# Modulation rows for GpSimd: four buffers in place of two, other places in the load order, and the gates' logarithm behind the first key chunk

## What is computed

```python
mod = silu(c) @ mod_w[l] + mod_b[l]              # 1024 x 6144, one row vector
sh1, sc1, g1, sh2, sc2, g2 = split(mod, 6)
h = rmsnorm(x, norm_g) * (1 + sc1) + sh1
proj = h @ w_in                                   # q, k: 512; v, og: 1024; gl: 16
log_a = log_sigmoid(gl @ w_g2 + b_g2) / 16        # the gates' logarithm
b = cumsum(log_a)                                 # inside chunks of 64 tokens
q_t, k_t, k_dec = q * exp(b), k * exp(-b), k * exp(b_last - b)
y = (chunked attention, normed, * silu(og)) @ w_out
x = x + g1 * y
h = rmsnorm(x, norm_g) * (1 + sc2) + sh2          # and so on
```

## Time and profile before

| | |
|---|---|
| median of 3 runs | 3109.04 us (3103.89 to 3110.97) |
| profiled execution | 3110.73 us, span 3108.9 us |
| PE busy | 2952.2 us, 95% |
| DVE busy | 2079.2 us, 67% |
| ACT busy | 1598.0 us, 51% |
| POOL busy | 1342.1 us, 43% |
| granted PE clock, mean | 0.974 |

### The profile page before, as it was taken

How to read it: one execution, slowest core, us unless ns; L and a number is a source line. 1 busy time by engine, 2 the same in 40 slices (tenths; PEclk the granted TensorE clock), 3 DMA queues, 4 the chain that set the end, 5 groups by cost and what they waited for, 6 DMA issues and landing times.

```text
span 3108.9 us, 59282 instructions
## 1 busy us (share of the span) xinstructions
PE 2952.2 (95%) x19024; PEld 2681.0 (86%) x19024; DVE 2079.2 (67%) x3812; ACT 1598.0 (51%) x3132; POOL 1342.1 (43%) x1069
## 2 busy tenths in 40 slices
PE   7999999988999998999999899999899999999998
PEld 6679999986787877899999777887799889999997
DVE  7646963358888877589203888888655447777776
ACT  1225554478555555555555865554564335455554
POOL 5823988886544410069888855444000010000100
PEclk8999999999999998999999999999999999999998
DMA  6534556731666632445567046665454345555553
GB/s 243 213 101 152 182 196 245 275 122 54 250 233 229 232 123 72 131 156 183 181 207 257 24 150 254 238 232 193 135 181 133 120 131 192 194 190 201 189 195 122
DMA packets 153464, 552.60 MB, mean 178 GB/s; under 512 B 16896, under 2 KB 19712, under 8 KB 153232
## 3 DMA queue, kind: packets, MB, share of 16 engines
q1 hardware_dynamic: 151136, 547.42, 51.5%
q10 hardware_dynamic: 2224, 3.87, 0.4%
HBM read 550.17 MB, written 1.05 MB: 177 GB/s over the span
## 4 chain that ended last, share of the span: by engine, by line
PE 60%; issue 20%; POOL 9%; ACT 7%; DVE 3%; DMA 1%; POOLq 0%; ACTq 0%; SPq 0%; DVEq 0%
PE bank L1002 20%; PE bank L1282 12%; PE bank L1032 10%; PE bank L1303 6%; PE bank L743 5%; ACT hT L1514 3%; PE bank L795 3%; POOL w_parts L2642 1%; POOL mean L2690 1%; POOL hT L2690 1%; ACT hT L1510 1%; POOL mean L2692 1%; POOL hT L2692 1%; ACT h_parts L1522 1%; PE bank L767 1%
## 5 line engine op out<-in xcount | busy, mean ns | idle before, releaser
L2642 POOL TENSOR_TENSOR w_parts<-ring,w_parts 128x512 fp32r<-128x512 f32 x512 | 660.9, 1308 | 419.3 <-ACT w_parts L1474 392.0
L1002 PE MATMUL bank<-h_parts,w_parts 128*128 128x256 f32 x6144 | 750.1, 284 | 7.0 <-POOL w_parts L2642 7.0
L1002 PEld LDWEIGHTS bank<-h_parts,w_parts 128*128 128x128 f32 x6144 | 741.7, 192 | 8.0 <-POOL w_parts L2642 5.5
L1474 ACT ACTIVATE w_parts<-ring 128x512 fp32r<-128x512 f32 x512 | 320.0, 631 | 343.3 <-PE bank L1002 238.1
L1695 ACT ACTIVATE w_parts<-ring 128x512 fp32r<-128x512 f32 x384 | 242.3, 632 | 266.0 <-PE bank L1282 171.2
L1282 PEld LDWEIGHTS bank<-h_parts,w_parts 128*128 128x128 f32 x3072 | 374.5, 193 | 3.9 <-DVE arena L2504 1.5
L1282 PE MATMUL bank<-h_parts,w_parts 128*128 128x256 f32 x3072 | 375.4, 284 | 1.4 <-DVE arena L2504 1.4
L1032 PE MATMUL bank<-w_parts,a_parts 128*128 128x512 f32 x1536 | 372.2, 398 | 2.4 <-DVE a_parts L2278 2.3
L2573 DVE TENSOR_TENSOR w_parts<-ring,w_parts 128x512 fp32r<-128x512 f32 x376 | 272.5, 736 | 147.5 <-ACT w_parts L1695 144.1
L1032 PE MATMUL bank<-h_parts,a_parts 128*128 128x512 f32 x1536 | 364.1, 392 | 6.6 <-DVE a_parts L2278 6.6
L1032 PEld LDWEIGHTS bank<-h_parts,a_parts 128*128 128x128 f32 x1536 | 285.2, 188 | 78.8 <-DVE a_parts L2278 20.6
(11 more groups left out here) (348 smaller groups left out, 4302.6 us busy)
## 6 DMA issues: line engine op xcount, KB each, us to landing
ring<-stream SPq DMA_DIRECT2D x786, 512.0 KB, 3.4
arena<-stream SPq DMA_DIRECT2D x144, 512.0 KB, 4.4
hT<-stream SPq DMA_DIRECT2D x80, 512.0 KB, 4.5
mean<-stream SPq DMA_DIRECT2D x32, 512.0 KB, 4.5
arena<-consts ACTq DMA_DIRECT2D x1, 1536.0 KB, 6.4
xT<-xin ACTq DMA_DIRECT2D x1, 1024.0 KB, 10.8
out<-hT SPq DMA_DIRECT2D x4, 256.0 KB, 2.2
arena<-subk ACTq DMA_DIRECT2D x2, 128.0 KB, 2.2
```

Of the source, the lines that this page charges most:

```text
L1002: mm = pe.matmul(bank[k][:, 0:T], w[:, wp, ws], h_parts[:, hp, 4 * j + q, :], start=(j == 0 and q == 0 and i == 0), stop=(j == 1 and q == ...
L1474: act.activation(w_parts[half % HALVES][:, 0, :], ring[slot_][:, j * 512:(j + 1) * 512], ACT.Copy).then_inc(sem(f"{n}_high"), 1)
L2642: pool.tensor_tensor(w[:, 1, :], ring[(base + k) % RING][:, j * 512:(j + 1) * 512], w[:, 0, :].bitcast(F32), ALU.subtract).then_inc(sem(f" ...
```

## The change

The 24 rows of POOL get four buffers (at 0, 1, 5 and 6 x 1024 of the arena), each with its own semaphore. The later groups of rows keep two. The two new buffers are those of DVE's first products, so from the third row on the load waits until DVE has made all nine of its rows (`first_made`), and from the fifth on it waits until the row four before it is made. In the list `at` the rows stand behind slots 17, 18, 19, 21, 22, 23, 25, ... (three rows for four slots) up to 42 for the twentieth, and the last four behind slot 43; before, they stood behind slots 8, 10, 14, 17, then two for three slots from 18 to 37, and six behind 43. In ACT's order the gates' sigmoid and logarithm come behind the eviction of the first key tile, not behind that of the fourth.

```diff
-        mod_landed = [sem("mod_landed0"), sem("mod_landed1")]
+        mod_landed = [sem(f"mod_landed{i}") for i in range(4)]
+        N_GLA = MODS_GLA[1] - MODS_GLA[0]
+
+        def mod_lane(j):
+
+            return j % 4 if j < N_GLA else j % 2
+
+        def mod_arrival(j):
+
+            return 16 * (j // 4 + 1) if j < N_GLA else 16 * ((j - N_GLA) // 2 + N_GLA // 4 + 1)
...
-                return arena[:, 0:CH], arena[:, CH:2 * CH]
+                return tuple(arena[:, i * CH:(i + 1) * CH] for i in (0, 1, 5, 6))
...
                 j = mod_number(m)
-                if m >= seg[0] + 2:
-                    sp.wait_ge(sem("mod_made"), j - 1)
-                sp.dma_start(mod_buffers(seg)[j % 2], stream[mod_row(m)]).then_inc(mod_landed[j % 2], 16)
+                lanes = len(mod_buffers(seg))
+                if m >= seg[0] + lanes:
+                    sp.wait_ge(sem("mod_made"), j - lanes + 1)
+                elif m >= seg[0] + 2:
+                    sp.wait_ge(sem("first_made"), len(SUMMED_MODS))
+                sp.dma_start(mod_buffers(seg)[mod_lane(j)], stream[mod_row(m)]).then_inc(mod_landed[mod_lane(j)], 16)
...
-            at = [8, 10, 14, gla + 1] + [gla + 2 + 3 * i // 2 for i in range(14)] + [gla + 27] * 6
+            at = [gla + 1 + 4 * i // 3 for i in range(20)] + [gla + 27] * 4
...
-            for h in range(GH):
-                copy_act(act, G.k[:, h, :], f"g_k{h}")
-
+            copy_act(act, G.k[:, 0, :], "g_k0")
             act.wait_ge(sem("g_abs"), 1)
             act.activation(G.e, G.e, ACT.Sigmoid, scale=-1.0).then_inc(signal("g_act"), 1)
             act.wait_ge(sem("g_act"), signalled("g_act"))
             act.activation(G.e, G.e, ACT.Ln).then_inc(signal("g_ln"), 1)
             act.wait_ge(sem("g_ln"), signalled("g_ln"))
+            for h in range(1, GH):
+                copy_act(act, G.k[:, h, :], f"g_k{h}")
...
-            pool.wait_ge(mod_landed[j % 2], 16 * (j // 2 + 1) if it is None else it * 32 + 16 * (j // 2 + 1))
+            pool.wait_ge(mod_landed[mod_lane(j)], mod_arrival(j) if it is None else it * 32 + mod_arrival(j))
```

More of the change, by code:

```diff
@@ L2684, in mod_pool @@
         def mod_pool(pool, seg, i, j, c_b, it=None):
-            buf, part = mod_buffers(seg)[j % 2], mod_parts(seg)[i % len(mod_parts(seg))]
+            buf, part = mod_buffers(seg)[mod_lane(j)], mod_parts(seg)[i % len(mod_parts(seg))]
             b3 = buf.rearrange("p (k n) -> p k n", k=DC)
             step = lambda k: 3 * j + k if it is None else it * 12 + (3 * j + k)
-            pool.wait_ge(mod_landed[j % 2], 16 * (j // 2 + 1) if it is None else it * 32 + 16 * (j // 2 + 1))
+            pool.wait_ge(mod_landed[mod_lane(j)], mod_arrival(j) if it is None else it * 32 + mod_arrival(j))
             pool.tensor_tensor(b3, b3, c_b, ALU.mult).then_inc(sem("mod_step"), 1)
```

## The result

| | before | changed |
|---|---|---|
| median | 3108.35 us (20 runs, 3102.19 to 3114.98) | 3117.73 us (20 runs, 3109.22 to 3123.31) |
| ratio | | 1.0028, 95% interval 1.0020 to 1.0035 |
| span of the profiled execution | 3108.9 us | 3117.2 us |
| granted PE clock, mean | 0.974 | 0.971 |

The forecast was 3104.8, between 3098 and 3111, with 6% for slower. The time lies outside the range and on the other side.

What follows compares the result with a forecast made beforehand. POOL's last row was taken to bound the output projection's start, at 178.9 instead of 183.10. The 4.2 us gained gave 3106.5 for the profiled execution and 3104.8 for the median, range 3098 to 3111.

Steps and rivals of the forecast that it cites:

- (a): Head, without POOL rows or loads: VectorE's first rows done 8.9 us earlier, first projection at 43.1 instead of 53.19.
- (b): Rope arguments after the norm: VectorE queues behind POOL, TensorE waits 3.5 us at the fourth query tile, plus 1.7 clock.
- (c): Four buffers for POOL's rows: its seventh row starts at 78.3, and from there POOL has no gap.
- (d): Gates' logarithm moved earlier: price and gain 0; without it VectorE's chain would end at 138, still ahead of TensorE.
- (e): POOL's last 18 rows: 81.7 us alone, 15.7 more beside VectorE's chain, 0.8 for later operations; last row at 176.5.
- (f): Gate projection: slot 40 lands at 135.1, TensorE wants it at 135.6, so the stall at 133.7 is gone.
- The sum: Output projection: TensorE could start at 173.3, POOL allows 178.9; the later counts, gaining 4.2 us on 183.10.
- my rivals: Four alternatives: no rope wait (0.27), POOL no bound (0.06), first projection unmoved (0.10), POOL ending at 178 to 180.
- Rival 3: First projection does not move, so POOL's late start is pure loss: 5.9 us later, 3114.9; chance 0.10.
- the heart of the case: Before the output projection: TensorE finishes POOL's last columns, then waits 1.77 us for VectorE, a margin of 1.8 us.

Runs made afterwards that it cites:

- e1: Changed kernel with VectorE's two scalings of the output gates moved behind its first four state copies; ratio to the kernel before 1.0012.
- e7: Kernel before with only the gates' logarithm moved behind the first key eviction; ratio to the kernel before 0.9999.
- e4: Changed kernel with the gates' logarithm put back behind the fourth key eviction; ratio to the kernel before 1.0012.
- e2: Changed kernel with seven useless 256-column matmuls on TensorE ahead of the state loop's second chunk, where it waits; ratio to the kernel before 1.0003.
- e6: Changed kernel with ScalarE's rope sines behind its first five evictions and VectorE's output-gate scalings behind the first state copies; ratio to the kernel before 0.9983.
- e10: Kernel before with only VectorE's output-gate scalings moved behind the first state copies; ratio to the kernel before 1.0002.
- e3: Kernel before with two extra maxima on VectorE between the output-gate scalings and the first state copies, to make TensorE wait; ratio to the kernel before 1.0050.
- e5: Changed kernel with ScalarE's two rope sines put behind its first five evictions; ratio to the kernel before 1.0008.

## Why the prediction was wrong, step by step

*(a) The head* was right: 8.9 us forecast, 10.1 with the gain operation, 9.2 to 11.4 measured (the upper bound was 11).

*(b) The rope collision* was right in its mechanism, and mis-sized. Of the 19 operations 14 met POOL, one for one; the first ran just ahead, and four in POOL's gap. This is VectorE in the changed kernel:

```profile
47.30 2.90 DVE L1954 SCALAR_TENSOR_TENSOR arena<-arena 128x256 f32<-128x256 f32 x3
50.23 1.87 DVE L1896 TENSOR_SCALAR arena<-arena 128x256 f32<-128x256 f32 x1
...
55.00 0.29 DVE L1900 TENSOR_SCALAR arena<-arena 128x256 f32<-128x256 f32 x1
...
56.31 2.00 DVE L1898 TENSOR_TENSOR rope_c<-rope_c,arena 128x256 f32<-128x256 f32 x1
```

An operation that takes 0.29 us in POOL's gap takes 1.87 behind POOL's longest one. The wait was forecast at 3.5 us and was 4.7 to 7.9. It has these two sizes because POOL's fourth row lands in the middle of the last operations: in e1 it lands after a gap of 0.67 us and catches six, in the changed kernel after 1.33 and catches four. I had three. With four caught the arguments were ready 19.2 us behind the start of the first projection, forecast 18.9; most of the 1.2 us over the forecast is that TensorE asked for the bank after 16.0 us and not after 16.9. With six caught, the wait is 7.8 to 7.9, beyond my bound (five caught, 2 us more).

*(c), (d)* were right in their own terms: POOL waited for no load behind the start of its seventh row (78.6, forecast 78.3), and the logarithm alone is worth nothing in the kernel before (e7). Without this edit the chain would have ended at 144.2 and not at my 138 (e4), 1 us before TensorE asked for it. But I looked at the end of VectorE's chain only, and its place decides also which of POOL's operations stands where the scalings begin (e4).

*(e) POOL's total.* The last 18 rows take 98.3 to 98.5 us in all six profiles with this load order and the sines in their old place; 98.2 was forecast. The last row came at 176.9 in the profiled execution of the changed kernel (forecast 176.5) and at 179.3 to 182.4 in the other five, since the seventh row started anywhere from 78.6 to 84.1, by the wait of (b) and by the start of the first projection. The profiled one had the earliest start of the six, 41.75 where 43.1 was forecast, so that its last row fits so well is in part luck. Behind it the last columns take 3.9 us and not 2.4, since a TensorE that waits for POOL does them at 1.2 GHz. POOL's bound is then at 180.8 to 186.3 and not at 178.9; e1, e2 and e4 show 183.2 and 186.3, which is no gain over 183.10.

*(f)* was right: no stall, or 1 us at most, at the gate projection.

*The sum* is where it failed: "could start the output projection 34.3 later". I took TensorE's path behind the gate projection over from the kernel before, at full clock, and it took 51.1 us (138.93 to 190.02). In (e) I had put 0.8 us of contention on POOL for VectorE's later operations, these scalings among them, and had not asked what the meeting costs VectorE, nor who waits for VectorE there. The price in the profiled execution was copies 2.1 us late, 1.5 us of wait, and 13.5 us in the state loop through the clock (0.9 and some 11 in its two other profiles); the 8 us or so that TensorE had to spare ahead of POOL's last row (8.06 of wait in e1) hid a part of it. Even without this loss nothing of the forecast gain of 4.2 us is left (e1, e2 and e4: 1.0003 to 1.0012), through the wait of (b) and the last columns of (e). Of the changed kernel's 8.7 us (0.28%), e1 gives back 5.0 and e6 another 9, more than all of it.

None of my rivals was this one. Rival 3, the only one on the slower side, has the first projection unmoved, and it moved about as forecast. What I called the heart of the case, POOL's margin of 1.8 us, was real but second.

The Trainium skill (SBUF — State Buffer, Who interferes with whom) has the rule that issue order decides who blocks; the trace agrees both times (1.87 us behind POOL, and POOL's 512-element halving at 1.59 in place of 1.27 us behind a scaling). It spoke against this change at the scalings as it did at the rope work, and I applied it only at the latter.

## What to carry to other kernels

When work is moved beside an engine whose operations meet its own one for one, as POOL's and VectorE's do here, go through every operation of the partner in the new stretch and ask who waits for it within a microsecond, not only through the long chain. A gap of one microsecond on TensorE cost 12 to 15 us here, with narrow matmuls behind it: price such a gap with the clock for the whole stretch behind, or keep work without a waiter (here the scalings) out of the place between a product and the copy that the next product needs. And look at what stands idle before: POOL's idle time before the change was also what kept it out of VectorE's way.

## What the runs showed of the hardware that I had not expected

The state loop ran at either clock. Without a wait it ran at 2.4 GHz in all ten profiles that have none (before, e1, e2 with its filler, e4 to e10); after 0.86 to 2.97 us of idle at its second chunk it ran at 1.2 GHz for 27 to 34 us, with TensorE busy all the time by the profile, and came back only around the 256-column matmuls that end the stage (the three profiles of the changed kernel, e3). But the dip of e5, from 142.0 to 145.3, began without a wait and ended among matmuls of 64 columns, so neither a wait nor the width alone is the rule. At the gate projection of the kernel before, with 256 columns, the wait of 3.09 us cost less: the granted clock was 0.50 for some 3 us and 1.00 again from 139.9 on. The Trainium skill (TensorE: Matmul & The Clock Gate, Part 1) ties the lower clock to an idle TensorE; here it fell behind idle times of 0.86 and 0.90 us among narrow matmuls, and it did not rise for 27 us and more in which TensorE was never idle for long.
